# Attention output for two query tiles at a time, one in each half of the PE array's columns

## The reference, cut to what matters

```python
s = (jnp.einsum('bqhd,bkhd->bhqk', q_nope, k_nope)
     + jnp.einsum('bqhr,bkr->bhqk', q_rope, k_rope))
p = jax.nn.softmax(s.astype(jnp.float32) * ATTN_SCALE, axis=-1).astype(v.dtype)
return jnp.einsum('bhqk,bkhd->bqhd', p, v)      # the product that is changed
```

## Time and profile before

| | |
|---|---|
| median of 3 runs | 2034.09 us (2032.62 to 2034.77) |
| the profiled execution, its own time | 2033.28 us |
| its span | 2031.5 us |
| PE busy | 1956.4 us, 96% of the span |
| DVE, ACT, POOL busy | 1364.2, 991.3, 91.0 us |
| share of PE in the chain that ended last | 92% |

### The profile page before, as it was taken

The page is one execution under the profiler, slowest core; times in us unless marked ns, Lnnn a source line. Parts: engine busy times, 40 slices in busy tenths (PEclk is TensorE's granted clock), DMA queues, the critical chain, the costliest instruction groups (busy, mean ns, idle before and its releaser), DMA issues.

```text
span 2031.5 us, 24090 instructions
## 1 busy us (share of the span) xinstructions
PE 1956.4 (96%) x9008; PEld 1555.3 (77%) x9008; DVE 1364.2 (67%) x1590; ACT 991.3 (49%) x1098; POOL 91.0 (4%) x127
## 2 busy tenths in 40 slices
PE   6999999999899999989999989999999999999997
PEld 3785666667688888868788978888878887888886
DVE  5753434378577656455344458999889988988995
ACT  3423333222522223243433367777767776777774
POOL 0150000000000001002100000000000000000000
PEclk9999999999899999989999979999999999999997
DMA  9312112244245556413233379989989988899980
GB/s 367 127 71 83 42 73 79 91 172 165 94 168 187 193 176 231 187 63 135 83 115 136 114 290 352 357 348 358 349 310 348 357 348 320 348 357 348 360 314 23
DMA packets 72401, 438.76 MB, mean 216 GB/s; under 512 B 9184, under 2 KB 9952, under 8 KB 28000
## 3 DMA queue, kind: packets, MB, share of 16 engines
q1 hardware_dynamic: 60624, 394.18, 51.1%
q0 software_dynamic: 11664, 43.00, 6.1%
HBM read 436.09 MB, written 1.05 MB: 215 GB/s over the span
## 4 chain that ended last, share of the span: by engine, by line
PE 92%; DVE 3%; ACT 3%; issue 2%; DMA 0%; SPq 0%; ACTq 0%; DVEq 0%
PE ps L1617 12%; PE ps L1618 12%; PE ps L1619 12%; PE ps L2005 7%; PE ps L2007 7%; PE ps L2006 7%; PE ps L1850 6%; PE ps L2019 4%; PE ps L2023 4%; PE ps L2020 4%; PE ps L1801 2%; PE ps L1825 2%; PE ps L1760 2%; PE ps L1651 1%; PE ps L1730 1%
## 5 line engine op out<-in xcount | busy, mean ns | idle before, releaser
L1434 DVE TENSOR_TENSOR elo<-estage,ehi 128x2048 fp32r<-128x2048 f32 x264 | 605.0, 2292 | 75.8 <-ACT ehi L945 64.2
L945 ACT ACTIVATE ehi<-estage 128x2048 fp32r<-128x2048 f32 x264 | 505.2, 1914 | 51.6 <-PE ps L2023 47.4
L1617 PE MATMUL ps<-h_hi,whi 128*128 128x512 f32 (+1 forms) x960 | 371.0, 386 | 17.7 <-DVE h_lo L1092 8.8
L1618 PE MATMUL ps<-h_lo,whi 128*128 128x512 f32 (+1 forms) x960 | 347.9, 362 | 0.0
L1619 PE MATMUL ps<-h_hi,wlo 128*128 128x512 f32 (+1 forms) x960 | 347.7, 362 | 0.0
L2005 PE MATMUL ps<-ehi,xg_hi 128*128 128x512 f32 x704 | 286.0, 406 | 8.7 <-issue 6.3
L2007 PE MATMUL ps<-ehi,xg_lo 128*128 128x512 f32 x704 | 278.0, 395 | 0.0
L2006 PE MATMUL ps<-elo,xg_hi 128*128 128x512 f32 x704 | 277.3, 394 | 0.0
L1052 DVE TENSOR_TENSOR wlo<-stage,whi 128x2048 fp32r<-128x2048 f32 x79 | 181.2, 2295 | 98.0 <-ACT whi L687 98.0
L687 ACT ACTIVATE whi<-stage 128x2048 fp32r<-128x2048 f32 x79 | 150.8, 1909 | 164.9 <-PE ps L1619 163.9
L1617 PEld LDWEIGHTS ps<-h_hi,whi 128*128 128x128 f32 x960 | 184.2, 192 | 59.3 <-issue 20.5
(11 more groups left out here) (224 smaller groups left out, 2375.4 us busy)
## 6 DMA issues: line engine op xcount, KB each, us to landing
estage<-in_moe SPq DMA_DIRECT2D x264, 1024.0 KB, 4.9
stage<-in_split SPq DMA_DIRECT2D x79, 1024.0 KB, 4.9
gw<-in_mods POOLq DMA_DIRECT2D x80, 512.0 KB, 3.8
dw<-in_direct SPq DMA_DIRECT2D x36, 512.0 KB, 3.7
mw_b<-in_mods SPq DMA_DIRECT2D x8, 512.0 KB, 12.6
mw_a<-in_early SPq DMA_DIRECT2D x8, 512.0 KB, 14.1
xT<-in_x SPq DMA_DIRECT2D x1, 2048.0 KB, 7.8
gw<-in_cond_rows SPq DMA_DIRECT2D x1, 1024.0 KB, 5.4
```

The lines of the kernel that those rows point to most:

```text
L945: act.activation(ehi[:, w % SPLIT, :], estage[:, w % STAGE, :], ACT.Copy).then_inc(S("e_hi_done"), 1)
L1434: dve.tensor_tensor(elo[:, w % SPLIT, :], estage[:, w % STAGE, :], ehi[:, w % SPLIT, :], ALU.subtract)\
L1617: pe.matmul(out, hi, rhs_hi, start=first, stop=False)
L1618: pe.matmul(out, hi, rhs_lo, start=False, stop=False)
```

## The change

`values(n)` becomes `values_of_two(n)` for items n and n+1. For each 128 keys it issues two matmuls with the same 64 columns of v: item n writes partitions 0 to 63 of `ps[6]`, item n+1 partitions 64 to 127, at the same columns. A matmul of 64 weight columns whose output begins at partition 64 is placed in the upper half of the array's columns; the tile of the array has the size 128x64 before and after, the position (0, 64) is new. It runs in odd steps only, for items n-3 and n-2, and it stands ahead of `turn(n - 1)` and no longer behind it. `head_out` becomes two copies, one from each half of the partitions, so `br_a` counts twice per head.

```diff
-                dve.tensor_copy(br[at:at + 64, 0, h // 2, lc:T], ps[6][0:64, lc:T]).then_inc(S("br_a"), 1)
+                rows = br[at:at + 64, 0, h // 2, lc:T].rearrange("p (a x t) -> p a x t", x=2, t=P)
+                for x in range(2):
+                    dve.tensor_copy(rows[:, :, x, :], ps[6][64 * x:64 * x + 64, lc // 2:SEQ].rearrange("p (a t) -> p a t", t=P)).then_inc(S("br_a"), 1)
...
-            def values(n):
+            def values_of_two(n):
+
                 h, q, keys = todo_a[n]
-                pe.wait_ge(S("pT"), earlier("pT", layer) + n + 1)
+                pe.wait_ge(S("pT"), earlier("pT", layer) + n + 2)
...
-                        pe.wait_ge(S("br_a"), earlier("br_a", layer) + h)
+                        pe.wait_ge(S("br_a"), earlier("br_a", layer) + 2 * h)
                 for t in range(keys // P):
-                    ins = pe.matmul(ps[6][0:64, q * P:(q + 1) * P], v_rows(t)[:, h * VD:(h + 1) * VD],
-                                    pT[:, n % 2, t * P:(t + 1) * P], start=(t == 0), stop=(t == keys // P - 1))
-                ins.then_inc(S("pv"), 1)
+                    for x in range(2):
+                        ins = pe.matmul(ps[6][64 * x:64 * x + 64, q // 2 * P:q // 2 * P + P], v_rows(t)[:, h * VD:(h + 1) * VD],
+                                        pT[:, (n + x) % 2, t * P:(t + 1) * P], start=(t == 0), stop=(t == keys // P - 1))
+                ins.then_inc(S("pv"), 2)
...
+                if n >= 3 and n % 2 == 1:
+                    values_of_two(n - 3)
                 if 1 <= n <= len(todo_a):
                     turn(n - 1)
-                if n >= 2:
-                    values(n - 2)
```

More of the change, by code:

```diff
@@ L226 @@
     "s_full": _ITEMS, "max": _ITEMS, "neg_max": _ITEMS, "prob": _ITEMS, "rden": _ITEMS, "pn": _ITEMS,
-    "t_full": _ITEMS, "pT": _ITEMS, "pv": _ITEMS, "br_a": HEADS,
+    "t_full": _ITEMS, "pT": _ITEMS, "pv": _ITEMS, "br_a": 2 * HEADS,
     "gate": KD * BRANCHES, "o_full": KD * BRANCHES, "o_used": KD * BRANCHES, "y_add": 2 * KD,
@@ L1597, in _ @@
             if layer == 0:
-                pool.wait_ge(S("br_a"), HEADS)
+                pool.wait_ge(S("br_a"), 2 * HEADS)
                 pool.dma_start(gw[:, :, :], A["cond_rows"]).then_inc(S("cond_rows2"), 16)
@@ L1847, in branch @@
                 if m == BESIDE:
-                    pe.wait_ge(S("br_a"), earlier("br_a", layer) + HEADS)
+                    pe.wait_ge(S("br_a"), earlier("br_a", layer) + 2 * HEADS)
                 for k in range(KB):
```

## The result

The changed kernel takes 2007.38 us in the median of 4 runs (2000.70 to 2009.24), the kernel before on the same chip 2034.43 (2032.62 to 2034.81): ratio 0.9865, 95% interval 0.9853 to 0.9877, faster by 27 us. The profiled execution took 2008.40 us (span 2006.6) against 2033.28: 24.9 us less.

The account below looks back on a forecast made before the run. The prediction took PE to bound the kernel, busy all the time in both attention loops. Its terms, 8.4 - 1.9 + 14.8 = 21.3 us less, gave 2012.0 for the profiled execution and a median of 2012.8, range 2008 to 2030.

Parts of the forecast that it names:

- full overlap: Forecast case for values passes: both halves run together, 0.218 us per unit of four passes, 14.8 us saved; chance 0.40.
- a free place for the load of the other half: Sign for the forecast case: earlier loads waited for the same columns; the other half's place is free, so loads needn't wait.
- PE bounds the loops, and a gain there arrives at the end: Attention loops: PE busy all the time, transfers ahead in the experts, so the whole gain was expected at the end.
- Fewer visits: Attention loops: 24 unbroken runs of values passes instead of 46, each with a fixed price of 0.29 or 0.34; 8.4 us saved.
- The way in from a 512-column pass: Start of a visit behind a 512-column matmul: taken as 0.145 us, as behind a transpose, with bounds 0 and 0.195.
- The ends: Last visit of each layer: PE waits for ACT's two copies, 1.15 us instead of 0.20; 1.9 us lost in all.
- DVE at nothing: One DVE copy per head becomes two: nothing put in the sum; 4.5 us if idle time did not cover it.
- Two halves side by side: Values passes in both array halves: 80 units at 0.218 us saved, less 2.6 for unpartnered last passes; 14.8 us saved.
- the late load: Values passes: upper load waits for the lower half's second pass, 0.328 us a unit; 13.8 us less, 2020.3; chance 0.20.
- no overlap: Values passes: the halves take turns at 0.109 us a pass; 6.5 us less, 2027.6; chance 0.22.
- seen loads: Values passes: halves take turns and each first load of a half shows, 7.5 us; 2035.1, no change; chance 0.08.
- Rival 4: Values passes: each change of half drains PE, 136 x 0.145 us, 19.7 us lost; slower, 2047.3; chance 0.10.

Follow-up runs that it names:

- one_half: Changed kernel with both items of a visit in the lower half, item after item, one DVE copy per head: 2026.44 us, 6.9 less than the kernel before.
- more_visits: Changed kernel with each visit cut in two at the middle of the keys, transposes between: 2016.13 us, 17.3 less than the kernel before.
- wide: Kernel before with v loaded 128 columns wide, so the array's tile stays 128x128: 2018.09 us, 15.3 less than the kernel before.
- own_visits: Kernel before with its 46 visits, but odd items in the upper half and two DVE copies per head: 2033.11 us, ratio 0.9998.
- late_end: Changed kernel with each layer's last visit moved behind the first half of the next gate matmuls: 2001.67 us, 31.7 less than the kernel before.
- best: Changed kernel with each layer's last visit moved later and one visit per head in layer 0 (second buffer pair): 2000.30 us, ratio 0.9831.
- repeat_1: late_end with the 16 passes of layer 0's last visit issued twice: 2003.54 us, 29.7 less than the kernel before.
- repeat_3: late_end with the 16 passes of layer 0's last visit issued four times: 2009.26 us, 23.9 less than the kernel before.
- halves_in_turn: Changed kernel with a visit's two loops exchanged, all lower-half passes and then all upper-half ones: 2015.33 us, 18.0 less than the kernel before.

## Why the prediction was wrong

The time, 2007.38, lies 0.6 us below the range (2008 to 2030). The forecast, full overlap, is the case that came, its sum was too small. No row of before decided between it and the rivals; the reason it went by, a free place for the load of the other half, is borne out by loads that start together (four in 0.20 us).

- *PE bounds the loops, and a gain there arrives at the end*: right. PE waits nowhere new but at the two ends, and the parts outside the loops add 1.0 us to the gain in sum, though the part behind the second loop took 1.7 us.
- *Fewer visits, 8.4 us*: right. one_half gives 6.7 with the ends in it, 8.3 without their 1.6; more_visits and wide put a visit at 0.33 us on two further ways. The way in from a 512-column pass is the 0.145 taken. It is made as the trace had it: a drain of 0.09 us and a load that nothing hides, at a change of the tile's size. The page "TensorEngine Tiling (Array Packing)" of the Trainium skill, section "Key Properties", says that the mode drains and the tile does not; wide (0.33 us a visit gone with the change of size) agrees with the first, own_visits and the pairs with the second.
- *The ends, 1.9 us lost*: 1.6, since the distance is 1.01 us and not 1.15, where 0.20 is usual; late_end, which takes the wait away, gains the same 1.6. ACT's copies went back to back, 1.09 us for the two and not 1.2.
- *DVE at nothing*: right. The 32 copies take 0.28 to 0.43 us each, and PE waits for none.
- *Two halves side by side, 14.8 us*: this term failed in its size; it measured 17.2. It said that "in the 24 visits the last upper pass has no partner, which gives back 24 x 0.109 = 2.6". I had let the passes start in the program's order (lower, lower, upper, upper), so that the first of a visit and the last would stand alone. They don't: the first upper pass starts ahead of the second lower one, and lower and upper go in pairs from the first to the last. one_half against the changed kernel: 23.9 - 6.7 = 17.2 us, which is 80 x 0.218 = 17.4 less a hundredth of a microsecond a visit.
- *Rivals 1 to 3*: the late load, no overlap, seen loads: each is refuted by the 0.49 us for eight passes. *Rival 4* is refuted by the same and by own_visits.
- *What the text did not have*: an amount for what lies outside the loops, which it put at nothing. With 17.4 for the halves and 1.6 for the ends the sum is 8.4 - 1.6 + 17.4 = 24.2, which the loops (23.9) confirm; from the median of 2034.1 that leads to 2009.9, inside the range. The last 2.5 us to the measured median are outside the loops (1.0 in the profiled execution). No experiment shows what made them; they go with the granted clock. Of the four runs of the first measurement the one of 2000.70 us has a mean clock of 0.982 and those of 2008.40 and 2009.24 have 0.976, and in best, repeat_1 and repeat_3 too the shortest run has the highest. That the time fell out of the range, by 0.6 us, is therefore in part chance. Between two measurements of the same kernel this part changed by 1.5 us, and its runs scatter from 2000.7 to 2009.2 where those of the kernel before lie within 2.8 us. The bound of 2008 allowed nothing for it; it was made of a way in at no price, which isn't so.

Open: why the changed kernel scatters more than the kernel before, and what decides where the clock falls and whether it does behind a stop. The column "outside" goes with the time at half clock (the two kernels with 18 and 20 us less gain most). repeat_3 has 5.6 us less at half clock and loses 3.4 us, but 4.6 us of that are its two further stops.

## What to carry to other kernels

Matmuls of 64 weight columns, float32 here, can be laid side by side in the two halves of the array at no cost of their own, and take half their time; in the program leave no more than three passes between a pass and its partner. Price a visit of such matmuls between full-width ones by itself (0.33 us here) and gather them: with 46 visits the switches cost 15.5 us, nearly as much as the halves bring (17.2). And when a change moves work ahead of a long part that it does not touch, set its gain against the same points of two traces before believing the last 2 or 3 us of a median.

## What the runs showed of the hardware

- Two halves of the columns take passes in pairs, and their loads as well, although both use the same 128 rows: eight passes in 0.49 us, 0.109 us a pair once it runs. The Trainium skill, page "TensorE: Matmul & The Clock Gate", section "The mechanism", says in its list of what overlaps that loads do so with running matmuls only where the row groups differ, and that matmuls start strictly in the program's order. The traces differ on both (the 0.109 us a pair; halves_in_turn starts upper passes ahead of three lower ones that stand before them), so the measurement decides.
- PE started a pass of the other half past three waiting ones, and not past four (halves_in_turn: all of a visit of 8 paired, 0.60 us; a visit of 16 only from its fifth pass on, 1.51 us).
- A change between 128x64 and 128x128 costs 0.145 us (into a 64-column load or a transpose) or 0.20 us (into a 128-column load). The kernel before paid it although it packed nothing; with v loaded 128 columns wide nobody pays it.
- A stop of PE of 3.2 us in the experts' loop is followed by matmuls at 1.2 GHz in one kernel and at 2.4 GHz in another, with the same instructions on both sides of it.
- Every stop of PE in that loop (2.2 to 3.4 us, 26 in the twelve traces) goes with a transfer of 16 KB of the kind "instruction" on queue q8; two stops are at the two jumps back of the loop.
